# Gathering token rows for two experts at once, in rounded high and low products

## The reference

```
def moe_swiglu(x, router, wg, wu, wd):
    logits = (x @ router).astype(jnp.float32)
    top_val, top_idx = lax.top_k(logits, TOP_K)            # TOP_K = 2 of N_EXPERTS = 8
    top_w = jax.nn.softmax(top_val, axis=-1)
    gates = jnp.sum(jax.nn.one_hot(top_idx, N_EXPERTS) * top_w[..., None], axis=-2)
    y = jnp.zeros_like(x)
    for e in range(N_EXPERTS):
        y = y + gates[..., e:e + 1] * swiglu(x, wg[e], wu[e], wd[e])
    return y
```

## Time and profile before

| | |
|---|---|
| median of 3 runs | 2033.01 us (2032.62 to 2035.44) |
| the profiled execution: its time, its span | 2034.68 us, 2032.9 us |
| TensorE matmul, busy | 2001.4 us (98%) |
| TensorE weight loads, busy | 1761.3 us (87%) |
| VectorE, busy | 1496.4 us (74%) |
| ScalarE, busy | 1199.0 us (59%) |
| read from HBM | 482 MB |

### The profile page before, as it was taken

How to read it: one execution, slowest core, us unless ns; L and a number is a source line. 1 busy time by engine, 2 the same in 40 slices (tenths; PEclk the granted TensorE clock), 3 DMA queues, 4 the chain that set the end, 5 groups by cost and what they waited for, 6 DMA issues and landing times.

```text
span 2032.9 us, 36044 instructions
## 1 busy us (share of the span) xinstructions
PE 2001.4 (98%) x15296; PEld 1761.3 (87%) x15296; DVE 1496.4 (74%) x1311; ACT 1199.0 (59%) x1076; POOL 53.6 (3%) x36
## 2 busy tenths in 40 slices
PE   8999999999999999999999999999999999999998
PEld 6978999999998888899988888888888888888886
DVE  6656356765455766438578898888889889898896
ACT  5454453543343545445467777777777777777675
POOL 0003100000000001200000000000000000000000
PEclk9999999999999999999999999999999999999999
DMA  7432035444442322105459899898998989899895
GB/s 239 172 111 97 4 133 201 166 166 172 187 162 106 142 106 86 41 27 225 179 224 380 344 358 373 323 372 336 369 367 335 373 334 364 349 359 372 326 376 199
DMA packets 75038, 485.60 MB, mean 239 GB/s; under 512 B 13480, under 2 KB 14632, under 8 KB 17192
## 3 DMA queue, kind: packets, MB, share of 16 engines
q1 hardware_dynamic: 73816, 481.93, 61.3%
q10 hardware_dynamic: 1104, 1.92, 0.3%
HBM read 482.08 MB, written 1.74 MB: 238 GB/s over the span
## 4 chain that ended last, share of the span: by engine, by line
PE 92%; DVE 4%; ACT 2%; DMA 1%; issue 1%; POOL 0%; ACTq 0%; SPq 0%; DVEq 0%
PE PS L576 26%; PE PS L578 25%; PE PS L577 25%; PE PS L956 6%; DVE area L1910 1%; PE PS L1282 1%; PE PS L1291 1%; DVE WL L1910 1%; ACT WH L1442 1%; PE PS L914 1%; DMA ring<-in_weights 1%; PE PS L731 1%; DVE YEL L2515 0%; PE PS L1358 0%; PE PS L847 0%
## 5 line engine op out<-in xcount | busy, mean ns | idle before, releaser
L1910 DVE TENSOR_TENSOR WL<-ring,WH 128x2048 fp32r<-128x2048 f32 x410 | 934.4, 2290 | 218.0 <-ACT WH L1442 109.3
L1442 ACT ACTIVATE WH<-ring 128x2048 fp32r<-128x2048 f32 x336 | 643.1, 1916 | 158.5 <-PE PS L578 149.0
L576 PE MATMUL PS<-WH,XGH 128*128 128x512 f32 x896 | 353.7, 395 | 0.2 <-DVE XGL L1910 0.2
L578 PE MATMUL PS<-WL,XGH 128*128 128x512 f32 x896 | 349.7, 390 | 0.0
L577 PE MATMUL PS<-WH,XGL 128*128 128x512 f32 x896 | 349.1, 390 | 0.0
L578 PE MATMUL PS<-XL,WH 128*128 128x272 f32 (+1 forms) x704 | 202.5, 288 | 0.0
L1434 ACT ACTIVATE WH<-ring 128x2048 fp32r<-128x2048 f32 x74 | 141.3, 1910 | 102.0 <-PE PS L578 102.0
L578 PEld LDWEIGHTS PS<-WL,XGH 128*128 128x128 f32 x896 | 168.1, 188 | 35.8
L576 PEld LDWEIGHTS PS<-WH,XGH 128*128 128x128 f32 x896 | 168.3, 188 | 34.6 <-DVE WL L1910 0.5
L577 PEld LDWEIGHTS PS<-WH,XGL 128*128 128x128 f32 x896 | 168.4, 188 | 33.5
L576 PE MATMUL PS<-WH,HTH 128*128 128x512 f32 x448 | 176.7, 394 | 0.6
(11 more groups left out here) (350 smaller groups left out, 3432.7 us busy)
## 6 DMA issues: line engine op xcount, KB each, us to landing
ring<-in_experts SPq DMA_DIRECT2D x336, 1024.0 KB, 6.6
ring<-in_weights SPq DMA_DIRECT2D x114, 1024.0 KB, 6.9
ring<-in_weights SPq DMA_DIRECT2D x4, 576.0 KB, 4.4
ring<-in_weights SPq DMA_DIRECT2D x4, 512.0 KB, 4.0
cst<-in_consts SPq DMA_DIRECT2D x1, 1731.0 KB, 7.4
hT<-in_stream ACTq DMA_DIRECT2D x2, 544.0 KB, 7.0
out<-area SPq DMA_DIRECT2D x4, 256.0 KB, 2.0
bias_line<-lin SPq DMA_DIRECT2D x1, 672.0 KB
```

What stands on the lines that cost most here:

```text
L576: pe.matmul(o, lh, rh, start=first, stop=False, skip_group_check=True)
L578: return pe.matmul(o, lh, rl, start=False, stop=last, skip_group_check=True)
L1442: act.activation(WH[(BASE + j + 1) % 3][:, :], ring[b][:, 2048 * (j % 2):2048 * (j % 2) + 2048], ACT.Copy).then_inc(S("w_hi"), 1)
L1910: tt = lambda o, a_, b_, op: dve.tensor_tensor(o, a_, b_, op)
```

## The change

Token rows are now gathered for two experts at once. The rows are kept in two parts, `TOKH` (rounded) and `TOKL` (the rest), and the selection `PICK` holds the 0/1 columns of two experts side by side, 256 columns. A gather is four rounds, each 8 rounded matmuls of 256 columns into two banks: round 0 the high parts of channel groups 0 to 3, round 1 their low parts, rounds 2 and 3 the same for groups 4 to 7. Since `PICK` is 0 or 1 and each column picks one row, the high rounds give `XGH` and the low rounds `XGL`, and each needs only a copy: ScalarE copies rounds 0 and 2, VectorE rounds 1 and 3. In the loop all four rounds use banks 2 and 3, so a round waits for the copy of the round before it. The loop body now holds two experts (`odd` 0 and 1) and runs three times, and the last two experts stand behind it.

```diff
+        XGH, XGL = pinned("XGH", [P, 2, D], at_xn), pinned("XGL", [P, 2, D], at2 + 4 * 8448)
+        TOKH, TOKL = pinned("TOKH", [P, 2, D], at_xh), pinned("TOKL", [P, 2, D], at2 + 4 * KT * T)
+        PICK = pinned("PICK", [P, 2, 2, SLOTS], at_slots)
...
+        FIRST_BANKS = 0, 2, 6, 4
...
-            with eng.Fori(0, NE - 1) as e:
-                body(eng, e, e, 0, False)
-            body(eng, NE - 1, NE - 1, 0, True)
+            PAIRS = NE // 2
+            with eng.Fori(0, PAIRS - 1) as i:
+                body(eng, i * 2, i * 2, 0, False, 0, i)
+                body(eng, i * 2 + 1, i * 2 + 1, 0, False, 1, i)
+            body(eng, NE - 2, NE - 2, 0, False, 0, PAIRS - 1)
+            body(eng, NE - 1, NE - 1, 0, True, 1, PAIRS - 1)
...
-                for k in range(KT):
+            def gather_round(r, bank):
+                token = (TOKH, TOKL)[r % 2]
+                for i in range(4):
+                    k = 4 * (r // 2) + i
                     for t in range(2):
-                        ins = pe.matmul(PS[:, 2 + k // 4, (k % 4) * SLOTS:(k % 4 + 1) * SLOTS], hnT[:, t, k * P:(k + 1) * P],
-                                        SEL[:, t, :], start=(t == 0), stop=(t == 1))
+                        ins = round_product(PS[:, bank + i // 2, (i % 2) * 2 * SLOTS:(i % 2 + 1) * 2 * SLOTS], token[:, t, k * P:(k + 1) * P],
+                                            PICK[:, t, :, :].rearrange("p x s -> p (x s)"), t == 0, t == 1)
                 ins.then_inc(S("e_xg"), 1)
+
+            def gather_pair(p, r):
+
+                if r == 0:
+                    pe.wait_ge(S("e_sel"), p + 1)
+                elif r % 2:
+                    pe.wait_ge(S("e_xgh"), p * 2 + (r // 2 + 1))
+                else:
+                    pe.wait_ge(S("e_xgl"), p * 2 + 1)
+                gather_round(r, 2)
...
+                    if odd and not last and kind == "u" and f == FG - 1:
+                        gather_pair(p + 1, half)
...
                     if (kind, f, half) == ("d", FG - 2, 0):
                         turn_hidden(n, FG - 1)
-                        if not last:
-                            gather(n + 2)
+                    if odd and not last and (kind, f) == ("d", FG - 2):
+                        gather_pair(p + 1, 2 + half)
...
-                    gather(1, "router_pe")
+                    pe.wait_ge(S("e_sel"), 1)
+                    gather_round(0, FIRST_BANKS[0])
+                    pe.wait_ge(S("router_dve"), ROUTER["first_low"])
+                    gather_round(1, FIRST_BANKS[1])
+                    gather_round(2, FIRST_BANKS[2])
                     pe.wait_ge(S("router_dve"), ROUTER["rows_low"])
+                    gather_round(3, FIRST_BANKS[3])
+                    pe.wait_ge(S("e_xgh"), 1)
+                    pe.wait_ge(S("e_xgl"), 1)
...
+            def gathered_high(p, r, bank):
+                act.wait_ge(S("e_xg"), p * 4 + (r + 1))
+                act.activation(gathered_view(XGH, r), gathered_banks(bank), ACT.Copy).then_inc(S("e_xgh"), 1)
...
+                if odd and not last:
+                    at_half(events, "u", FG - 1, 0, 2).append((lambda r: gathered_high(p + 1, r, 2), 0))
+                    at_half(events, "d", FG - 2, 0, 2).append((lambda r: gathered_high(p + 1, r, 2), 2))
...
+                if odd and not last:
+                    at_half(events, "u", FG - 1, 1, 2).append((lambda r: gathered_low(p + 1, r, 2), 1))
+                    at_half(events, "d", FG - 2, 1, 2).append((lambda r: gathered_low(p + 1, r, 2), 3))
...
+            def gathered_low(p, r, bank):
+                dve.wait_ge(S("e_xg"), p * 4 + (r + 1))
+                dve.tensor_copy(gathered_view(XGL, r), gathered_banks(bank)).then_inc(S("e_xgl"), 1)
...
+            def token_low(q):
+
+                for t in range(2):
+                    cols = slice(512 * q, 512 * q + 512)
+                    ins = dve.scalar_tensor_tensor(TOKL[:, t, cols], PS[:, 2 + t + 2 * q, :], MR[:, 184 + t:185 + t], TOKH[:, t, cols].bitcast(F32),
+                                                   ALU.mult, ALU.subtract)
+                ins.then_inc(S("router_dve"), 1)
...
+                    dve.tensor_reduce(small[:, 41:42], PS[:, 6, 16:24], AX.X, ALU.max)
+                    dve.wait_ge(S("router_act"), ROUTER["rows"])
+                    token_low(0)
+                    token_low(1)
+                    gathered_low(0, 1, FIRST_BANKS[1])
+                    gathered_low(0, 3, FIRST_BANKS[3])
                     gate_weights()
```

More of the change, by code:

```diff
@@ L401, in build_trunk, with gathered_view, gathered_banks @@
         N_SETUP = 6
[L403 to L405 removed]
+        ROUTER = {"logits": 1, "squares": 2, "turned": 3, "rank": 4,
+                  "mean": 1, "selected": 2, "rstd": 3, "gap": 4, "first_low": 5, "rows_low": 6,
+                  "root": 1, "rows": 2, "exp": 3}
+        FIRST_BANKS = 0, 2, 6, 4
+        def gathered_view(x_, r):
+            return x_[:, :, 512 * (r // 2):512 * (r // 2) + 512].rearrange("p x (k s) -> p k x s", s=SLOTS)
+        def gathered_banks(b):
+            return PS[:, b:b + 2, :].rearrange("p h (k x s) -> p (h k) x s", x=2, s=SLOTS)
         block = ctx.enter_context(nc.Block())
@@ L447, in at_half, with expert_loads @@
             return events[min(first_half[(kind, f)] + half + later, HALVES - 1)]
-        def expert_loads(sp, e, n, run, last):
+        def expert_loads(sp, e, n, run, last, odd, p):
             for i in range(len(MOE_ORDER)):
@@ L471, in for_all_experts @@
                         before(eng, again + 1)
-                    with eng.Fori(0, NE - 1) as e:
-                        body(eng, e, again * NE + e + NE, again + 1, False)
-                    body(eng, NE - 1, again * NE + (2 * NE - 1), again + 1, True)
+                    with eng.Fori(0, PAIRS - 1) as i:
+                        for odd in range(2):
+                            body(eng, i * 2 + odd, again * NE + i * 2 + (NE + odd), again + 1, False, odd, again * PAIRS + i + PAIRS)
+                    for odd in range(2):
+                        body(eng, NE - 2 + odd, again * NE + (2 * NE - 2 + odd), again + 1, bool(odd), odd, again * PAIRS + (2 * PAIRS - 1))
                 if after:
@@ L1305, in half_products @@
                         x_, w_ = slice(k * SLOTS, (k + 1) * SLOTS), slice(i * 512, (i + 1) * 512)
-                        ins = three_products(o, XGH[:, x_], XGL[:, x_], WH[s_][:, w_], WL[s_][:, w_], k == 0, k == KT - 1)
+                        ins = three_products(o, XGH[:, odd, x_], XGL[:, odd, x_], WH[s_][:, w_], WL[s_][:, w_], k == 0, k == KT - 1)
                 else:
@@ L1326, in final_rows, with expert_products @@
                                       start=(k == 0), stop=False, is_transpose=True, skip_group_check=True)
-            def expert_products(pe, e, n, run, last):
-                pe.wait_ge(S("e_xgl"), n + 1)
+            def expert_products(pe, e, n, run, last, odd, p):
+                pe.wait_ge(S("e_xgh"), p * 2 + 2)
+                pe.wait_ge(S("e_xgl"), p * 2 + 2)
                 for j in range(1, HALVES):
@@ L1870, in first_highs @@
                     expert_high(run * NE, j)
-                if first:
-                    act.wait_ge(S("router_pe"), ROUTER["gathered"])
-                    act.activation(XGH[:, 0:512], PS[:, 2, :], ACT.Copy).then_inc(S("router_act"), 1)
-                    act.wait_ge(S("e_xg"), 1)
-                    act.activation(XGH[:, 512:D], PS[:, 3, :], ACT.Copy).then_inc(S("e_xgh"), 1)
-                else:
-                    gathered_high(act, run * NE + 1)
+                for r in (0, 2):
+                    gathered_high(run * (NE // 2), r, FIRST_BANKS[r] if first else 2)
                 for j in range(2 if first else 3, AHEAD):
@@ L2481, in add_expert, with expert_hidden @@
                 return tt(o, o, PS[:, (2, 6)[i]:(2, 6)[i] + 2, :].rearrange("p a (b n) -> p a b n", b=2), ALU.add)
-            def expert_hidden(dve, e, n, run, last):
+            def expert_hidden(dve, e, n, run, last, odd, p):
                 steps = 5
```

58 lines of the change are left out of this document (22 added, 36 removed).

## The result

The changed kernel takes 2051.16 us (median of 4 runs, 2049.55 to 2052.04) against 2034.22 for the kernel before (4 runs, 2032.62 to 2037.43) beside it: 1.0077 times as long, with a 95% interval of 1.0062 to 1.0092. That is about 16 us slower, where 10.4 us faster was forecast. The profiled execution took 2050.34 us with a span of 2048.5.

What follows compares the result with a forecast made beforehand. The prediction took the kernel as bound by what TensorE issues, with the weight stream second. Its terms, -25.0 + 11.4 + 1.35 + 0.45 + 1.4 = -10.4 us, took 2033.0 to 2022.6 us, range 2019.8 to 2028.0.

Steps and rivals of the forecast that it cites:

- Removed, 25.0 us: Expert stage: seven gathers of 3.57 us each leave TensorE's path, 25.0 us saved; the eighth, at the start, counted apart.
- 96 rounds' matmuls, 11.4 us: Three pair gathers in and behind the loop: 96 rounded 256-column matmuls at 0.119 us add 11.4 us on TensorE.
- Round 2 waits for `XGL`'s copy, 0.45 us a pair: Odd expert's end: TensorE waits for VectorE's copy of round 1, 0.2 us plus 0.25 for the restart, 1.35 in all.
- rival (d): VectorE's copies, with output jumping between two experts' places, run far slower, making the kernel slower; 2043 at 5 us; chance 0.03.
- rival (e): Gather rounds run at the unrounded price, 0.446 us a matmul, 42.8 us instead of 11.4, giving 2054; chance 0.01.
- `YEL` later, 0.45 us: Before the scatter: VectorE's `WL` work pushes `YEL` about 0.15 us later, three times, 0.45 us in all.
- The start, 0.7 and 0.8 us: Stage start: half 0 begins 0.7 us late, then TensorE pauses 0.8 for the flag (0.3 waiting, 0.5 reading).
- Rival (c), the weight stream: Weight loads set the pace at even experts' ends, 1 us in each of four, giving 2026.6; chance 0.06.
- Rival (b), the returns: The longer loop body is fetched again; TensorE stands 2.5 us at each of two returns, giving 2027.6; chance 0.14.
- The transfers change nothing in amount: Remark beside the sum: the change leaves the amount of data transferred as it was, with no time added.

Runs made afterwards that it cites:

- kernel 2: The kernel before with only `XGH` moved to `at_xn`, byte 59008, in its old one-expert shape: 2047.41 us, 1.0057.
- kernel 7: The changed kernel with `XGH` at `at2`, a multiple of 512, and its loop of pairs written out: 2023.93 us, 0.9945 of the kernel before.
- kernel 1: The changed kernel with only `XGH` moved to `at2`, byte 178688, a multiple of 512: 2041.48 us, 1.003 of the kernel before.
- Kernel 3: The changed kernel with its loop of pairs written out, `XGH` still at `at_xn`: 2037.06 us, 1.0015 of the kernel before.
- kernel 4: The kernel before with two experts in a loop body, each with its own gather, plus one tiny VectorE write: 2049.56 us, 1.0073.
- kernel 9: The kernel before with its loop of seven experts written out: 2032.75 us, 0.9988.
- kernel 5: The changed kernel with `XGH` at `at_xn + 384`, byte 59392, same region but a multiple of 512: 2040.85 us, 1.0025 of the kernel before.
- kernel 6: The changed kernel with `XGH` at `at2 + 128`, byte 178816, not a multiple of 512: 2054.07 us, 1.0086 of the kernel before.

## Why the prediction was wrong

Term by term, as the prediction put them.

- **Removed, 25.0 us**: right. No row of the unrounded gathers is left.
- **96 rounds' matmuls, 11.4 us**: right. Rounds 0, 1 and 3 take 0.95 to 0.96 us on the chain, as here at the end of one expert:

```profile
1265.63 0.96 PE PS L598 x8
...
1269.34 0.44 PE PS L1315 x4
1269.79 1.22 PE PS L598 x8
...
1273.76 0.95 PE PS L598 x8
```

- **Round 2 waits for `XGL`'s copy, 0.45 us a pair**: the mechanism was right, the size too large: 1.22 on the chain instead of 0.95, 0.27 us a pair and 0.8 in all instead of 1.35. The copy took what was worked out, 1.22 us, behind `hidden(6)`, in VectorE's timeline:

```profile
1267.92 0.68 DVE L1943 TENSOR_TENSOR area<-area,PS 128x512 f32<-128x512 f32 x1
1268.52 1.22 DVE L2594 CAST XGL<-PS 128x1024 fp32r<-128x1024 f32 x1
```

So rival (d), a slow copy, is refuted, and rival (e) by the round's 0.96.
- **`YEL` later, 0.45 us**: of no weight. The changed kernel waits 3.1 us in seven waits, against 3.6 before, but that is the slower products' doing: kernel 2, with nothing but the address, has 3.0. Kernel 7, with quick products, has 3.7, so 0.1 us later.
- **The start, 0.7 and 0.8 us**: from VectorE's selections (1026.30) to half 0 (1031.60) it is 5.30 us, against 1027.56 to 1032.22, 4.66, before: 0.64 later. The pause behind half 0 was 1.48 us instead of 0.8. The flag's last instruction starts at 1034.58 and takes 0.15, TensorE goes on at 1036.06: 1.3 us for reading and branching where 0.5 was taken; in kernel 7 the chain has 1.00. The Trainium skill's figure for a `tensor_load` ("DMA: Bandwidth & Descriptors", section "Latency and other measured facts") is a floor of about 0.6 us; the trace lies above it, as a floor allows.
- **Rival (c), the weight stream**: not in the changed kernel (6.5 us of ScalarE waits) and hardly in kernel 7 (26.2 us, 0.6 of them passed on to TensorE's weight loads). In the slowest execution of kernel 1 it cost TensorE 2.4 us, about the size that (c) had.
- **Rival (b), the returns**: this is the first step that failed. It was seen and given 0.14, against the argument that "code without loops runs through the first half of the kernel, and TensorE is 98% busy". Kernel 3 shows why that argument was none: straight code, with 39 fetches, has no pause, and a return to a long body does. Its price, 2.5 us a return, was too low by more than half: 5.35 and 4.40 us idle, within the bound of 6.6 that stood there, and 1.4 and 1.5 us of half clock, which the prediction didn't have. The Trainium skill ("Runtime: NRT & Kernel Launch", section "Instruction fetch mechanics") gives TensorE 2,048 instructions and lets a taken branch wait when its target is outside the window. The runs agree: a body of about 1,170 has no pause at its returns, and one of twice that has, in the changed kernel and in kernel 4. The same section puts the window at two pages of 256 instructions; by that the short body too would be fetched at every return, and the kernel before shows that it isn't, with no fetch on q8 from 1160 to 1920 us.
- **The place of `XGH`** is the second, and no term or rival had it. The diff's line with `at_xn` was read as a matter of room. The sentence "The transfers change nothing in amount", and a sum with nothing for the 4,032 products of the expert stage, took their rate for given. The runs showed 5.9 ns more from one gate or up product to the next, 14 to 15 us in all.

The stage in one sum: -25.0 + 11.4 + 0.8 for the rounds, + 0.1 for `YEL`, + 1.5 for the pause, + 12.7 for the returns, + 15.1 for the place (the stage of kernel 3, 994.4, less that of kernel 7, 979.3) = 16.6 us, against 1006.9 - 990.6 = 16.3. The terms of returns and place, 27.8, turned the forecast gain into a loss.

With both taken out, the rest of the prediction can be tested by itself, and it holds. Kernel 7 is 11.2 us faster than the kernel beside it (8.5 to 13.6), where 10.4 was forecast; writing the loop out alone gave 2.4 us in kernel 9, of which 0.4 in the stage. Its periods, from the first scatter matmul of one expert to that of the next, alternate between 124.8 us with a gather (1155.49 to 1280.26) and 120.6 without (1280.26 to 1400.81), where 125.0 and 120.6 were forecast.

Two sizes are known within bounds. The place costs 13.9 us of the stage in kernel 2, 15.1 from kernel 7 to 3 and 12.7 from kernel 5 to the changed one; in the runs' times it is 8 to 15 us by kernel 2's interval, 11 by kernel 6 against 1, and 14 by kernel 3 against 7. The returns cost 12.5 us of the stage from kernel 3 to the changed one, 14.9 from kernel 7 to 5, and 15.8 in kernel 4. Much of that spread is in the traces: the two pauses come to 9.75, 10.4 and 10.1 us, and the half clock behind them lasts for 15, 16 and 27 matmuls. Why it lasts longer in one execution than in another, no run tells.

## What to carry to other kernels

A change that lengthens a loop body is to be costed at the loop's return, by the instructions of the engine that bounds the kernel; if a short body has no pause, that says nothing of a long one, and writing the loop out is a cheap way to see it. A float32r buffer that TensorE loads as weights is best laid on a multiple of 256 bytes, the places that were quick here, and when a diff moves a buffer, its address modulo 256 is compared before anything else is. Where a kernel has thousands of equal matmuls, their median duration is the first thing to compare between two traces: 6 ns on 2,688 of them weighed as much as the whole saving of the seven gathers, 13.6 us.

## What the runs showed of the hardware

A float32r operand that TensorE loads as weights, 128 bytes off a multiple of 256, makes the 512-column matmuls that use it start 0.2335 us apart instead of 0.2276 (median 395 instead of 389 ns), in both regions tried (bytes 59008 and 178816); a multiple of 256 (178944) and multiples of 512 (59392, 178688, 212480) are alike. The weight loads' own records stay at 188 ns, and the matmuls with `XGL` between them, whose operand is on a multiple of 512, grow too. That the load is slower in truth and is covered by the matmul before it in the records was not shown.

A return to a body of about 2,350 TensorE instructions stops TensorE for 4.4 to 5.5 us beside a weight stream of 367 GB/s, at all twelve returns of the six kernels that have one, and one block of instructions comes in meanwhile. The clock behind it is granted at 0.50 for 7 to 14 matmuls. The same fetches in straight code cost nothing that the profile shows, and a body of about 1,170 that is run seven times isn't fetched again.
